# A decoder step on one core: norm weights spread by matmul, another load order for the first tile, bias rows read backwards, two small products moved later

## The chip, the cores and the metric

The kernel runs on one NeuronCore of one Trainium2 chip. Times are microseconds (us) of device time of one launch. The kernel before was run three times: 622.79, 621.86 and 620.78 us, median 621.86 us. One further execution was profiled.

## What is computed

The reference is one inference step of a hybrid decoder layer, on 512 prompt rows and 8 x 4 sample rows (544 rows in all, 1,024 wide). The part that the change touches is cut out here; after it come the gating mixer, the merge and the final norm.

```python
def rmsnorm(x, g):
    y = xf * lax.rsqrt(jnp.mean(xf * xf, axis=-1, keepdims=True) + EPS)
    return (y * g).astype(x.dtype)

h = rmsnorm(x, norm_g)                       # norm_g: 1024 weights
proj = jnp.einsum('bsd,de->bse', h, w_in)    # q, k, v, gates, ...
s_own = qf @ k_own + table_t[:, rel_bucket(pos_i[:, None] - own_pos[None, :])]
# causal attention of the prompt with a bias by distance (32 buckets per head)
# block-sparse attention of the sample rows over a paged cache, same table
```

## The kernel before, in words

All five engines run programs written out by hand; semaphores tie them together.

**The front (up to about 26 us).** The SP queue loads five row tiles of x (`XR`, 128 rows each, the last one 32 rows), and between them the norm weights copied to all 128 partitions (`GBC`, 512 KB, line 352), the constants (`CST`, line 353) and the first two pairs of weight tiles (`load_w(0)`, `load_w(1)`, 1 MB each). For each row tile r, ACT sums the squares (line 812), DVE makes the mean (`mean_square`, line 1011), POOL the inverse root (line 1399), DVE multiplies by it and by `GBC` (`normalise`, line 1018), PE transposes it in eight 128-column pieces (`turn_x(u)`, two u per tile, line 495), ACT copies the result out as `XH` (`x_hi`, called through line 799) and DVE makes the rest `XL` (`x_lo`, line 1027). Three tiles are made ready before the first projection half starts; `turn_x(6)` to `turn_x(9)`, tiles 3 and 4, are woven into that half. `turn_x(u)` waits for `x_lo` of u-4, whose PSUM bank it takes over. DVE's own order is ms(0), norm(0), ms(1), norm(1), ms(2), x_lo(0), norm(2), x_lo(1), x_lo(2), then tiles 3 and 4. Every weight tile is split in a high part `WH` (ACT, `split_hi`) and a low part `WL` (DVE, `split_lo`; for tiles 0 and 1 POOL, line 1409).

**The 12 tiles of q, k and v (26 to 112 us).** For tile n, PE runs `half(n, 0)`, then small extra work, then `half(n, 1)`. A half is 24 matmuls of 272 columns (line 455). ACT evicts each half. The extra work: at n=1 the table products; at n=5 to 11 `rows(n-1)`, five transposes of k or v; at n=5 and 6 two `flip` products each (line 517, FLIP x TREV, 128x512 f32), which ACT copies to `TPH`; at n=9 the local scores of the sample rows; at n=10 a wait for `loc_ok` and one product with `SUM` (line 553). `TREV` holds bias rows that POOL wrote to HBM and loads back with a step of one element per partition (lines 1411 to 1414). After the loop PE runs `rows(11)` and waits for `lmx_ok`.

**The steps (112 to about 500 us).** 144 steps t, ordered by hand: each transposes a page of keys (line 575), runs four k-steps of the remaining projection (`run(fill, 2)` twice) and adds page scores, page values and the pieces of prompt attention. `prompt_max` (DVE, lines 1177 to 1187) adds `TPH` to the scores in PSUM (line 1182) and takes the maximum; it runs 16 times, two adds each. The mixing, merge and final norm follow.

Of the kernel before, what the change touches and what calls it, by code (L numbers as in the profile page):

```python
# [8 lines left out]
F32 = mybir.dt.float32  # L9
# [71 lines left out]
C_ID, C_SUM, C_OWN, C_PAIR, C_TRI, C_FLIP = 0, 128, 256, 260, 262, 326  # L81
C_KEPT = 326
C_COLS = 454
# [6 lines left out]
def constants():  # L90

    c = np.zeros((P, C_COLS), np.float32)
    row, col = np.arange(P)[:, None], np.arange(P)[None, :]
    c[:, C_ID:C_ID + P] = np.eye(P)
    c[:, C_SUM:C_SUM + P] = row % 32 == col % 32
    c[:, C_FLIP:C_FLIP + P] = row + col == P - 1
# [7 lines left out]
    i[:, I_EVEC:I_EVEC + VLEN] = onehot([255 - u for u in range(VLEN)])  # L104
    i[:, I_VMASK:I_VMASK + VLEN] = np.where(np.arange(VLEN) > 255, NEG, 0.0)
# [39 lines left out]
def build(nc, x_p, x_s, cache_k, cache_v, page_table, rel_bias, norm_g, w_in, ln_g, ln_b, w_s, b_s, w_pa, w_pb,  # L145
          w_o, fin_g, cst, ini, sgc, y_p, y_s, k_p, v_p, k_s, v_s, sgu_s):
    with ExitStack() as ctx:
# [36 lines left out]
        CST = sb("CST", [P, C_KEPT])  # L184
# [46 lines left out]
        TREV = at("TREV", [P, NH, 2 * P], F32, o); o += NH * 2 * P * 4  # L231
        FLIP = at("FLIP", [P, P], F32, o); o += P * 4
# [46 lines left out]
        cst_ld, ini_ld, pt_ld, gbc_ld = sem("cst_ld"), sem("ini_ld"), sem("pt_ld"), sem("gbc_ld")  # L279
# [5 lines left out]
        tb_ok, tab_pe, tab_ok, vec_st, trev_ld = sem("tb_ok"), sem("tab_pe"), sem("tab_ok"), sem("vec_st"), sem("trev_ld")  # L285
        flip_ld, flip_pe, tph_ok = sem("flip_ld"), sem("flip_pe"), sem("tph_ok")
# [41 lines left out]
        def _(sp):  # L328
# [17 lines left out]
            for r in range(5):  # L346
                if r < 4:
                    sp.dma_start(XR[:, r, :], x_p[0, r * P:(r + 1) * P, :]).then_inc(x_ld[r], 16)
                else:
                    sp.dma_start(XR[0:NSR, r, :], x_s.rearrange("b t d -> (b t) d")).then_inc(x_ld[r], 16)  # L350
                if r == 0:
                    sp.dma_start(GBC[:], bass.AP(norm_g.tensor, norm_g.offset, [[0, P], [1, DM]])).then_inc(gbc_ld, 16)
                    sp.dma_start(CST[:], cst[:, 0:C_KEPT]).then_inc(cst_ld, 16)
                if r == 2:
                    load_w(0)
# [3 lines left out]
            sp.dma_start(FLIP[:], cst[:, C_FLIP:C_FLIP + P]).then_inc(flip_ld, 16)  # L359
# [84 lines left out]
        def _(pe):  # L444
# [41 lines left out]
            pe.wait_ge(cst_ld, 16)  # L486

            def turn_x(u):
                r, kk = u // 2, u % 2
                n = P if r < 4 else NSR  # L490
                wait(pe, xn_ok, r + 1)
                wait(pe, xt_lo, u - 3)
                for j in range(4):
                    k = 4 * kk + j
                    last = pe.transpose(BK[4 + u % 4][:, j * n:(j + 1) * n], XR[0:n, r, k * P:(k + 1) * P], IDN[0:n, 0:n])
                last.then_inc(xt_pe, 1)
# [12 lines left out]

            def flip(x):  # L510

                if x == 0:
                    pe.wait_ge(trev_ld, 16)
                    pe.wait_ge(flip_ld, 16)
                    pe.wait_ge(tab_ok, 1)
                wait(pe, tph_ok, x - 1)
                mm(BK[2 + x % 2][:], FLIP[:], TREV[:, 2 * x:2 * x + 2, :], start=True, stop=True).then_inc(flip_pe, 1)

# [3 lines left out]
            for n in range(N_QKV):  # L522
# [17 lines left out]
                if n in (5, 6):  # L540
                    flip(2 * (n - 5))
                    flip(2 * (n - 5) + 1)
                if n == 9:

                    pe.wait_ge(qc_ok, 4)
                    pe.wait_ge(tph_ok, 4)
                    for b in range(NB):
                        for c in range(PAIRS):
                            last = mm(BK[3][0:32, b * 32:(b + 1) * 32], QC[:, b, c, :], KTS[:, c, SEQ:ROWS], start=(c == 0), stop=(c == PAIRS - 1))
                    last.then_inc(loc_pe, 1)  # L550
                if n == 10:
                    pe.wait_ge(loc_ok, 1)
                    mm(BK[2][:, 0:NB], SUM, LMX0[:], start=True, stop=True).then_inc(lmx_pe, 1)
                run(half(n, 1))
            rows(N_QKV - 1)
# [173 lines left out]
            for t in range(STEPS):  # L729
                if t < PAGES:  # L730
                    turn_page(t)
                run(fill, 2)
                if t % 4 == 0 and 4 <= t <= PAGES:
                    page_scores(t // 4 - 1)
# [62 lines left out]
        def _(act):  # L797
# [3 lines left out]
            def split_hi(n):  # L801
                m = n // 2
                act.wait_ge(w_ld[m % 2], w_need(m))
# [18 lines left out]
            squares(1)  # L822
            x_hi(0)
            squares(2)
            x_hi(1)
            split_hi(0)
# [6 lines left out]
            for n in range(N_QKV):  # L833
# [146 lines left out]
        def _(dve):  # L980
# [25 lines left out]
            dve.wait_ge(zero_ok, 7)  # L1006
# [6 lines left out]
            def normalise(r):  # L1013
                n = P if r < 4 else NSR
                if r == 0:
                    dve.wait_ge(gbc_ld, 16)
# [50 lines left out]
            for n in range(N_QKV):  # L1067
# [13 lines left out]
                if n == 11:  # L1081
# [3 lines left out]
            rows_out(N_QKV - 1)  # L1085
# [88 lines left out]
            def prompt_max(i):  # L1174
# [3 lines left out]
                if i == 0:  # L1178
                    dve.wait_ge(tph_ok, 4)
# [107 lines left out]
            for t in range(STEPS):  # L1287
                n = N_QKV + t // 4
                if t % 4 == 0 and 4 <= t <= 128:
# [101 lines left out]
        def _(pool):  # L1391
# [9 lines left out]
            pool.wait_ge(zero_ok, 7)  # L1401
# [12 lines left out]
            pool.dma_start(TREV[:], bass.AP(vec_d.tensor, vec_d.offset, [[1, P], [VLEN, NH], [1, 2 * P]])).then_inc(trev_ld, 16)  # L1414
# [42 lines left out]
```

## Time and profile before

| | |
|---|---|
| three runs | 622.79, 621.86, 620.78 us (median 621.86) |
| profiled execution, its own time | 621.19 us |
| its span in the trace | 618.9 us |
| PE busy | 576.7 us (93%) |
| DVE, ACT, POOL busy | 314.6, 215.2, 33.1 us |
| DMA | 112.50 MB, mean 182 GB/s |

The execution's time is 2.3 us above its span; what lies around the span is the same program start and end in every run. A busy time is a sum over the span, and an engine that is not the bound may idle at no cost. The chain that ended last is followed back from the last instruction, at each step to what released it. Line numbers are those of the kernel before.

### The profile page before, as it was taken

What the parts mean: (1) busy time and instruction counts of PE and PEld (TensorE: products, weight loads), DVE (VectorE), ACT (ScalarE), POOL (GpSimd) and SP (SyncE); (2) the same over time, 40 slices, a digit from 0 to 9 for tenths busy, and PEclk for the clock granted to TensorE, in tenths of its full rate; (3) what the DMA queues carried; (4) which work ended last, traced back from release to release, by engine and by line L of the source; (5) the groups of instructions that cost most, each with busy time, mean ns of one, the idle gap of its engine ahead of it and who ended that gap; (6) DMA issues with size and microseconds to landing.
All of it is one profiled execution on the core that took longest, in us unless ns stands there. A gap on an engine that the chain in (4) does not pass through costs nothing.

```text
span 618.9 us, 15227 instructions
## 1 busy us (share of the span) xinstructions
PE 576.7 (93%) x6242; PEld 540.6 (87%) x6242; DVE 314.6 (51%) x695; ACT 215.2 (35%) x466; POOL 33.1 (5%) x42
## 2 busy tenths in 40 slices
PE   3899998999999999999999989999999999979990
PEld 2799998999899899999889978989999989979990
DVE  5532223436446555655855745873642455952306
ACT  5422322332433434444544442232443231323213
POOL 1310120100000000000000000020000001100002
PEclk9999999999999999999999999999999999989996
DMA  8337332564775866767658578786798572332003
GB/s 296 115 106 253 104 117 93 190 173 126 228 227 183 242 202 191 219 207 226 203 173 254 173 231 256 240 257 181 218 341 298 169 245 70 121 127 69 1 1 144
DMA packets 73990, 112.50 MB, mean 182 GB/s; under 512 B 5417, under 2 KB 38194, under 8 KB 73922
## 3 DMA queue, kind: packets, MB, share of 16 engines
q1 hardware_dynamic: 72690, 108.18, 55.1%
q0 software_dynamic: 1232, 3.36, 1.7%
q8 instruction: 50, 0.82, 0.6%
q14 instruction: 18, 0.15, 0.1%
HBM read 106.98 MB, written 4.53 MB: 180 GB/s over the span
## 4 chain that ended last, share of the span: by engine, by line
PE 75%; DVE 15%; ACT 5%; issue 3%; DMA 2%; SPq 0%; POOL 0%; DVEq 0%; ACTq 0%; POOLq 0%
PE BK L455 46%; PE BK L575 7%; PE BK L587 4%; PE BK L601 4%; PE BK L475 3%; PE BK L651 2%; DVE WL L997 2%; DVE G L1278 1%; PE BK L668 1%; PE BK L658 1%; ACT WH L799 1%; DVE XR L1018 1%; ACT SC L897 1%; ACT FJ L976 1%; DMA SGC<-in_gating_constants 1%
## 5 line engine op out<-in xcount | busy, mean ns | idle before, releaser
L455 PE MATMUL BK<-XH,WH 128*128 128x272 f32 x704 | 223.7, 318 | 1.4 <-DVE XL L1027 1.4
L455 PE MATMUL BK<-XH,WL 128*128 128x272 f32 x704 | 204.1, 290 | 0.0
L455 PE MATMUL BK<-XL,WH 128*128 128x272 f32 x704 | 203.0, 288 | 0.0
L455 PEld LDWEIGHTS BK<-XH,WH 128*128 128x128 f32 x704 | 133.2, 189 | 12.2 <-issue 9.2
L455 PEld LDWEIGHTS BK<-XL,WH 128*128 128x128 f32 x704 | 133.8, 190 | 0.5 <-issue 0.5
L455 PEld LDWEIGHTS BK<-XH,WL 128*128 128x128 f32 x704 | 133.1, 189 | 0.0
L997 DVE TENSOR_TENSOR WL<-WRAW,WH 128x1024 fp32r<-128x1024 f32 x56 | 68.6, 1224 | 100.7 <-ACT WH L799 100.6
L575 PE MATMUL BK<-CST,KRAW 128*128 128x128 f32 x512 | 77.1, 273 | 2.4 <-DVE ATS L1171 2.2
L1091 DVE COPY KT<-BK 128x512 f32<-128x512 f32 x64 | 44.2, 691 | 57.1 <-PE BK L575 57.0
L799 ACT ACTIVATE WH<-WRAW 128x1024 fp32r<-128x1024 f32 x60 | 63.2, 1053 | 18.0 <-PE BK L475 18.0
L575 PEld LDWEIGHTS BK<-CST,KRAW 128*128 128x128 f32 x512 | 60.2, 140 | 4.4 <-issue 4.1
L455 PE MATMUL BK<-MH,WH 128*128 128x272 f32 x128 | 37.8, 295 | 3.9 <-issue 3.9
L799 ACT ACTIVATE KT<-BK 128x512 f32<-128x512 f32 x64 | 38.1, 595 | 4.3 <-PE BK L575 3.1
L455 PE MATMUL BK<-MH,WL 128*128 128x272 f32 x128 | 37.6, 294 | 0.0
L455 PE MATMUL BK<-ML,WH 128*128 128x272 f32 x128 | 37.4, 292 | 0.0
L587 PE MATMUL BK<-KT,QC 128*32 128x128 f32 x1024 | 34.6, 276 | 0.0
L799 ACT ACTIVATE G<-BK 128x272 f32<-128x272 f32 x32 | 12.7, 397 | 62.3 <-PE BK L455 62.1
L601 PE MATMUL BK<-VRAW,PT 128*32 128x128 f32 x960 | 31.8, 273 | 0.1
L1399 POOL TENSOR_TENSOR RSTD<-MS,NHALF 128x1 f32<-128x1 f32 (+1 forms) x15 | 10.8, 722 | 373.0 <-DVE MS L1234 292.1
L587 PEld LDWEIGHTS BK<-KT,QC 128*32 128x32 f32 x1024 | 26.0, 109 | 4.8 <-issue 1.1
L910 ACT ACTIVATE APX<-BK,NMX 128x128 f32<-128x128 f32 (+3 forms) x32 | 16.6, 522 | 34.2 <-DVE NMX L1187 34.2
L455 PEld LDWEIGHTS BK<-MH,WH 128*128 128x128 f32 x128 | 24.8, 193 | 4.1 <-issue 4.1
(186 smaller groups left out, 776.6 us busy)
## 6 DMA issues: line engine op xcount, KB each, us to landing
KRAW<-in_cache_k SPq DMA_DIRECT2D x128, 256.0 KB, 3.5
VRAW<-in_cache_v SPq DMA_DIRECT2D x120, 256.0 KB, 3.7
WRAW<-in_w_in SPq DMA_DIRECT2D x22, 1024.0 KB, 5.7
WRAW<-in_w_o SPq DMA_DIRECT2D x4, 1024.0 KB, 5.1
XR<-in_x_prompt SPq DMA_DIRECT2D x4, 512.0 KB, 6.4
VEX<-in_cache_v SPq DMA_DIRECT2D x8, 256.0 KB, 4.6
WRAW<-in_w_pb SPq DMA_DIRECT2D x4, 512.0 KB, 6.8
WRAW<-in_w_pa SPq DMA_DIRECT2D x4, 512.0 KB, 5.2
```

The costliest lines, as they stand in the source:

```text
L455: last = mm(BK[h][:, 0:HALF], w[:, n % 2, k, :], x[:, k, cols], start=(k == 0 and w is WH and x is XA), stop=(k == KC - 1 and w is WL))
L475: last = mm(bank[:, 0:HALF], w[:, n % 2, 4 * x + k, :], y[:, k, cols], start=(k == 0 and w is WH and y is XA), stop=(k == 3 and w is WL))
L575: last = pe.transpose(BK[2 + i % 2][:, c * P:(c + 1) * P], KRAW[:, i % KR, c * P:(c + 1) * P], IDN)
L587: last = mm(SCB[32 * j:32 * j + 32, x * P:(x + 1) * P], QC[:, b, c, :], KT[:, (4 * q + j) % KB, c, :], start=(c == 0), stop=(c == PAIRS - 1))
L601: last = mm(OUT[32 * c:32 * c + 32, 0:P], PT[:, x, 32 * j:32 * j + 32], vals[:, c * P:(c + 1) * P], start=(p == 0), stop=False)
L651: last = mm(BK[6 + e][:, k0:k1], QT[hd, c, y * P:(y + 1) * P], KTS[hd, c, k0:k1], start=True, stop=True)
L658: last = pe.transpose(BK[6 + e][:, j * P:(j + 1) * P], APX[:, e, j * P:(j + 1) * P], IDN)
L799: return act.activation(o, i, ACT.Copy)
L910: act.activation(APX[:, e, 0:n], BK[6 + e][:, 0:n], ACT.Exp, bias=NMX[:, e:e + 1], scale=1.0 / UNIT, accum_out=PLS[:, e:e + 1]).then_inc(a ...
L997: dve.tensor_tensor(WL[:, n % 2], WRAW[:, n // 2 % 2, :, n % 2 * P:(n % 2 + 1) * P], f32(WH[:, n % 2]), ALU.subtract).then_inc(w_lo, 1)
L1091: dve.tensor_copy(KT[:, i % KB], BK[3][:].rearrange("p (c n) -> p c n", c=PAIRS)).then_inc(kt_dve, 1)
L1399: pool.tensor_tensor(RSTD[0:n, r:r + 1], MS[0:n, r:r + 1], NHALF[0:n], ALU.pow).then_inc(done, 1)
```

## The change

- `norm_g` is loaded once, as one row `GROW` of 4 KB on one partition. PE multiplies a column of ones with it (`ONE`, 1x128, against two halves of 1x512) into banks 6 and 7, DVE copies both to `GBC`. Both stand ahead of everything else on PE and DVE; `turn_x(2)` waits for the copies.
- The constants are loaded in two parts (identity early, the rest late). The loads are in the order x0, GROW, identity, x1, x2, first half of the first weight pair, x3, sample rows, the other half, `load_w(1)`, and the small tables.
- On ACT, `squares(2)` goes ahead of `x_hi(0)` and `split_hi(0)` ahead of `x_hi(1)`. On DVE, `x_lo(0)` goes behind `normalise(2)`.
- `FLIP`, `TREV` and the four flip products with their ACT copies are gone. The bias rows are written in the other order and loaded straight into `TPH`; `prompt_max` reads them with a step of -1.
- The `loc_ok` wait and the product with `SUM` go from n=10 to n=11, and `rows(11)` from the end of the loop into step 0, behind its first two k-steps; DVE's `rows_out(11)` goes with it.

```diff
-            for r in range(5):
-                ...
-                if r == 0:
-                    sp.dma_start(GBC[:], bass.AP(norm_g.tensor, norm_g.offset, [[0, P], [1, DM]])).then_inc(gbc_ld, 16)
-                    sp.dma_start(CST[:], cst[:, 0:C_KEPT]).then_inc(cst_ld, 16)
-                if r == 2:
-                    load_w(0)
+            def load_x(r):
+                sp.dma_start(XR[:, r, :], x_p[0, r * P:(r + 1) * P, :]).then_inc(x_ld[r], 16)
+            load_x(0)
+            sp.dma_start(GROW[:], norm_g).then_inc(g_ld, 16)
+            sp.dma_start(CST[:, 0:P], cst[:, 0:P]).then_inc(id_ld, 16)
+            load_x(1)
+            load_x(2)
+            c = COLUMN[0] * P
+            sp.dma_start(WRAW[:, 0, :, 0:P], w_in[0, :, c:c + P].rearrange("(k p) n -> p k n", p=P)).then_inc(w0_ld, 16)
+            load_x(3)
+            sp.dma_start(XR[0:NSR, 4, :], x_s.rearrange("b t d -> (b t) d")).then_inc(x_ld[4], 16)
+            sp.dma_start(WRAW[:, 0, :, P:2 * P], w_in[0, :, c + P:c + 2 * P].rearrange("(k p) n -> p k n", p=P)).then_inc(w_ld[0], 16)
             load_w(1)
             sp.dma_start(INI[:], ini).then_inc(ini_ld, 16)
             sp.dma_start(TAB[:], rel_bias).then_inc(ini_ld, 16)
-            sp.dma_start(FLIP[:], cst[:, C_FLIP:C_FLIP + P]).then_inc(flip_ld, 16)
+            sp.dma_start(CST[:, P:], cst[:, P:]).then_inc(cst_ld, 16)
...
-            pe.wait_ge(cst_ld, 16)
+            pe.wait_ge(g_ld, 16)
+            pe.wait_ge(zero_ok, 8)
+            for x in range(2):
+                last = mm(BK[6 + x][:], ONE[:], GROW[:, 512 * x:512 * x + 512], start=True, stop=True)
+            last.then_inc(gbc_pe, 1)
+            pe.wait_ge(id_ld, 16)
...
+                if u == 2:
+                    pe.wait_ge(gbc_ok, 1)
...
-                if n in (5, 6):
-                    flip(2 * (n - 5))
-                    flip(2 * (n - 5) + 1)
                 if n == 9:
                     pe.wait_ge(qc_ok, 4)
-                    pe.wait_ge(tph_ok, 4)
+                    pe.wait_ge(tab_ok, 1)
...
-                if n == 10:
+                if n == N_QKV - 1:
                     pe.wait_ge(loc_ok, 1)
+                    pe.wait_ge(cst_ld, 16)
                     mm(BK[2][:, 0:NB], SUM, LMX0[:], start=True, stop=True).then_inc(lmx_pe, 1)
                 run(half(n, 1))
-            rows(N_QKV - 1)
             pe.wait_ge(lmx_ok, 1)
...
                 run(fill, 2)
+                if t == 0:
+                    rows(N_QKV - 1)
...
             squares(0)
             squares(1)
+            squares(2)
             x_hi(0)
-            squares(2)
+            split_hi(0)
             x_hi(1)
-            split_hi(0)
...
-                if n in (5, 6):
-                    for x in (2 * (n - 5), 2 * (n - 5) + 1):
-                        act.wait_ge(flip_pe, x + 1)
-                        copy(TPH[:, 2 * x:2 * x + 2, :], BK[2 + x % 2][:].rearrange("p (h n) -> p h n", h=2)).then_inc(tph_ok, 1)
...
-            dve.wait_ge(zero_ok, 7)
+            dve.memset(ONE[:], 1.0).then_inc(zero_ok, 1)
+            dve.wait_ge(zero_ok, 8)
+            dve.wait_ge(gbc_pe, 1)
+            for x in range(2):
+                last = dve.tensor_copy(GBC[:, 512 * x:512 * x + 512], BK[6 + x][:])
+            last.then_inc(gbc_ok, 1)
...
             for r in range(3):
                 mean_square(r)
-                if r == 2:
-                    x_lo(0)
                 normalise(r)
+            x_lo(0)
             x_lo(1)
...
-                    add = dve.tensor_tensor(bk[:, n - w:n], bk[:, n - w:n], TPH[:, 2 * c + e, 2 * P - w:2 * P], ALU.add)
+                    bias = TPH[:, 2 * c + e, 0:w]
+                    add = dve.tensor_tensor(bk[:, n - w:n], bk[:, n - w:n], bass.AP(bias.tensor, bias.offset + w - 1, [list(bias.ap[0]), [-1, w]]), ALU.add)
...
-            pool.dma_start(TREV[:], bass.AP(vec_d.tensor, vec_d.offset, [[1, P], [VLEN, NH], [1, 2 * P]])).then_inc(trev_ld, 16)
+            pool.dma_start(TPH[:], bass.AP(vec_d.tensor, vec_d.offset + 1, [[1, P], [VLEN, NH], [1, 2 * P]])).then_inc(tph_ld, 16)
```

## Rows read from the trace of the kernel before

**Rows 1.** The page: busy time of PE, and its clock in 40 slices (tenths).

```profile
PE 576.7 (93%) x6242; PEld 540.6 (87%) x6242; DVE 314.6 (51%) x695; ACT 215.2 (35%) x466; POOL 33.1 (5%) x42
...
PEclk9999999999999999999999999999999999989996
```

**Rows 2.** The chain that ended last, 0 to 36 us: start us, us, what.

```profile
0.76 3.63 DMA XR<-in_x_prompt
...
6.63 1.29 DVE XR L1018
...
8.06 1.96 PE BK L495 x8
...
11.86 1.20 DVE XL L1027 x2
...
14.30 1.98 PE BK L495 x8
...
20.78 3.39 DVE XR L1018
...
25.96 6.99 PE BK L455 x54
```

**Rows 3.** Timeline of the front: start us, us, engine, line, operation [idle before, releaser].

```profile
1.21 0.42 SPq L352 DMA_DIRECT2D GBC<-in_norm_g  x1
...
8.16 1.06 ACT L812 ACTIVATE JUNK<-XR 128x1024 f32<-128x1024 f32 x1 [2.60 <-DMA XR<-in_x_prompt]
...
9.34 0.15 DVE L1011 TENSOR_SCALAR MS<-SS 128x1 f32<-128x1 f32 x1 [1.42 <-ACT JUNK L812]
...
10.16 1.28 DVE L1018 SCALAR_TENSOR_TENSOR XR<-XR,RSTD,GBC 128x1024 f32<-128x1024 f32 x1 [0.67 <-POOL RSTD L1399]
...
14.00 1.05 ACT L799 ACTIVATE WH<-WRAW 128x1024 fp32r<-128x1024 f32 x1
...
17.68 0.59 PE L455 MATMUL BK<-XH,WH 128*128 128x272 f32 x1 [1.41 <-DVE XL L1027]
...
20.72 2.35 POOL L1409 TENSOR_TENSOR WL<-WRAW,WH 128x1024 fp32r<-128x1024 f32 x1
```

**Rows 4.** Two matmuls of the projection before 20 us and two after 24.5 us, same timeline.

```profile
18.08 0.43 PE L455 MATMUL BK<-XL,WH 128*128 128x272 f32 x1
...
18.30 0.43 PE L455 MATMUL BK<-XH,WL 128*128 128x272 f32 x1
...
24.80 0.29 PE L455 MATMUL BK<-XL,WH 128*128 128x272 f32 x1
...
24.93 0.29 PE L455 MATMUL BK<-XH,WL 128*128 128x272 f32 x1
```

**Rows 5.** DMA issues, 0 to 70 us: KB each, us from issue to landing.

```profile
GBC<-in_norm_g SPq DMA_DIRECT2D x1, 512.0 KB, 5.2
...
TAB<-in_rel_bias SPq DMA_DIRECT2D x1, 1.0 KB, 9.0
...
vec_scratch<-VEC POOLq DMA_DIRECT2D x1, 12.0 KB, 1.9
```

**Rows 6.** The chain again, 54 to 72 us, around the flip products.

```profile
59.94 1.72 PE BK L517 x4
...
68.25 1.72 PE BK L517 x4
```

**Rows 7.** Timeline of DVE at 60 us: a copy of one PSUM bank.

```profile
59.97 0.69 DVE L1060 COPY RS<-BK 128x512 f32<-128x512 f32 x1 [0.98 <-PE BK L508]
```

**Rows 8.** Who PE waited for, 56 to 125 us: us in total, times, longest.

```profile
PE BK L553 <- DVE LMX L1080: 1.7, 1, 1.7
PE BK L507 <- issue: 0.5, 1, 0.5
```

**Rows 9.** Line 1182, duration ns min/median/max; and the chain, 186 to 200 us.

```profile
L1182 DVE TENSOR_TENSOR BK<-BK,TPH x32: 289/423/433, 154.3 to 344.3; 128x256 f32<-128x256 f32 x24, 128x128 f32<-128x128 f32 x8
...
191.59 0.77 DVE BK L1182 x2
```

More of the change, by code:

```diff
@@ L78, in onehot @@
     return e
-C_ID, C_SUM, C_OWN, C_PAIR, C_TRI, C_FLIP = 0, 128, 256, 260, 262, 326
-C_KEPT = 326
-C_COLS = 454
+C_ID, C_SUM, C_OWN, C_PAIR, C_TRI = 0, 128, 256, 260, 262
+C_COLS = 326
 I_E15, I_ELOC, I_EVEC, I_VMASK, I_LOCM = 0, 512, 640, 1024, 1408
@@ L95, in constants @@
     c[:, C_SUM:C_SUM + P] = row % 32 == col % 32
-    c[:, C_FLIP:C_FLIP + P] = row + col == P - 1
     c[:, C_OWN:C_OWN + 4] = np.arange(4)[None, :] == row // 32
@@ L103, in constants @@
         i[:, I_ELOC + t * 32:I_ELOC + (t + 1) * 32] = onehot([t - j for _ in range(NB) for j in range(TD)])
-    i[:, I_EVEC:I_EVEC + VLEN] = onehot([255 - u for u in range(VLEN)])
-    i[:, I_VMASK:I_VMASK + VLEN] = np.where(np.arange(VLEN) > 255, NEG, 0.0)
+    i[:, I_EVEC:I_EVEC + VLEN] = onehot([u - P for u in range(VLEN)])
+    i[:, I_VMASK:I_VMASK + VLEN] = np.where(np.arange(VLEN) < P, NEG, 0.0)
     m = np.full((NH, TD, NB, NB, TD), NEG, np.float32)
@@ L183, in build @@
         TG = sb("TG", [P, 2, ROWS])
-        CST = sb("CST", [P, C_KEPT])
+        CST = sb("CST", [P, C_COLS])
         PTB = sb("PTB", [1, PAGES], I32)
@@ L230, in build @@
         VEC = at("VEC", [NH, VLEN], F32, o); o += VLEN * 4
-        TREV = at("TREV", [P, NH, 2 * P], F32, o); o += NH * 2 * P * 4
-        FLIP = at("FLIP", [P, P], F32, o); o += P * 4
+        GROW = at("GROW", [1, DM], F32, o); o += DM * 4
+        ONE = at("ONE", [1, P], F32, o); o += P * 4
         assert o <= g_at + 24 * ROWS * 4
@@ L278, in build @@
         x_ld = [sem(f"x_ld{r}") for r in range(5)]
-        cst_ld, ini_ld, pt_ld, gbc_ld = sem("cst_ld"), sem("ini_ld"), sem("pt_ld"), sem("gbc_ld")
+        id_ld, cst_ld, ini_ld, pt_ld, g_ld, w0_ld = (sem(n) for n in ("id_ld", "cst_ld", "ini_ld", "pt_ld", "g_ld", "w0_ld"))
+        gbc_pe, gbc_ok = sem("gbc_pe"), sem("gbc_ok")
         w_ld = [sem("w_ld0"), sem("w_ld1")]
@@ L284, in build @@
         xt_pe, xt_hi, xt_lo = sem("xt_pe"), sem("xt_hi"), sem("xt_lo")
-        tb_ok, tab_pe, tab_ok, vec_st, trev_ld = sem("tb_ok"), sem("tab_pe"), sem("tab_ok"), sem("vec_st"), sem("trev_ld")
-        flip_ld, flip_pe, tph_ok = sem("flip_ld"), sem("flip_pe"), sem("tph_ok")
+        tb_ok, tab_pe, tab_ok, vec_st, tph_ld = sem("tb_ok"), sem("tab_pe"), sem("tab_ok"), sem("vec_st"), sem("tph_ld")
         w_hi, w_lo, pj = sem("w_hi"), sem("w_lo"), sem("pj")
@@ L344, in load_w @@
                     sp.dma_start(WRAW[:, slot], w_in[0, :, c:c + 2 * P].rearrange("(k p) n -> p k n", p=P)).then_inc(w_ld[slot], 16)
-            for r in range(5):
[L347 to L350, printed above, removed]
-                if r == 0:
-                    sp.dma_start(GBC[:], bass.AP(norm_g.tensor, norm_g.offset, [[0, P], [1, DM]])).then_inc(gbc_ld, 16)
-                    sp.dma_start(CST[:], cst[:, 0:C_KEPT]).then_inc(cst_ld, 16)
-                if r == 2:
-                    load_w(0)
+            def load_x(r):
[10 more added lines that the diff above has]
+            sp.dma_start(WRAW[:, 0, :, P:2 * P], w_in[0, :, c + P:c + 2 * P].rearrange("(k p) n -> p k n", p=P)).then_inc(w_ld[0], 16)
             load_w(1)
@@ L508, in rows @@
                 pe.transpose(bs[0:NSR, 0:P], src[:, SEQ:ROWS], IDN).then_inc(rows_pe, 1)
[L510 to L517, printed above, removed]
             for u in range(6):
@@ L802, in split_hi @@
                 m = n // 2
-                act.wait_ge(w_ld[m % 2], w_need(m))
+                if n == 0:
+                    act.wait_ge(w0_ld, 16)
+                else:
+                    act.wait_ge(w_ld[m % 2], w_need(m))
                 wait(act, pj, matmuls_before(n - 1) if n > 1 else 0)
@@ L1015, in normalise @@
                 if r == 0:
-                    dve.wait_ge(gbc_ld, 16)
+                    dve.wait_ge(gbc_ok, 1)
                 dve.wait_ge(rstd_ok, r + 1)
@@ L1080, in _ @@
                     dve.tensor_reduce(LMX0[0:32, :], LOCS[:], AX.X, ALU.max).then_inc(loc_ok, 1)
-                if n == 11:
+                if n == N_QKV - 1:
                     dve.wait_ge(lmx_pe, 1)
@@ L1084, in _ @@
                 split_lo(n + 2)
-            rows_out(N_QKV - 1)
             def page_out(i):
@@ L1178, in prompt_max @@
                 if i == 0:
-                    dve.wait_ge(tph_ok, 4)
+                    dve.wait_ge(tph_ld, 16)
                 for e in range(2):
                     bk = BK[6 + e]
-                    add = dve.tensor_tensor(bk[:, n - w:n], bk[:, n - w:n], TPH[:, 2 * c + e, 2 * P - w:2 * P], ALU.add)
+                    bias = TPH[:, 2 * c + e, 0:w]
+                    add = dve.tensor_tensor(bk[:, n - w:n], bk[:, n - w:n], bass.AP(bias.tensor, bias.offset + w - 1, [list(bias.ap[0]), [-1, w]]), ALU.add)
                 link(add)
@@ L1288, in _ @@
                 n = N_QKV + t // 4
+                if t == 0:
+                    rows_out(N_QKV - 1)
                 if t % 4 == 0 and 4 <= t <= 128:
@@ L1399, in inverse_root @@
                 pool.tensor_tensor(RSTD[0:n, r:r + 1], MS[0:n, r:r + 1], NHALF[0:n], ALU.pow).then_inc(done, 1)
-            pool.wait_ge(zero_ok, 7)
+            pool.wait_ge(zero_ok, 8)
             for r in range(5):
```

## The prediction

> **What bounds the kernel now.** I read the page first. PE is busy for 93% of the span, and the clock line shows 9 tenths or more in nearly every slice [rows 1], so from about 26 us on anything that takes PE instructions away, or an idle gap of PE, should come off the time almost one for one, and work on DVE, ACT or POOL matters only where PE waits for it. The exception is the start. I followed the chain of waits there and then the timeline beside it: until the first projection matmul at 17.68 us [rows 3] the chain goes load of the first x tile, squares, root, norm on DVE, transposes on PE, and again [rows 2]. PE is mostly idle there; the last wait of the front is for the norm of the sample rows (3.39 us from 20.78), and from 25.96 us PE runs without a gap [rows 2]. A change of the front counts only by what it does to this chain. The other two views are the chain around the flip products [rows 6] and the list of what PE waited for up to 125 us, which has just two entries in the stretch that the change touches [rows 8].
>
> **Term 1, the flip products.** Each of the two groups stands on the chain with 1.72 us [rows 6], between two runs of line 455. Removing them gives 2 x 1.72 = 3.44 us. Their four ACT copies and the two loads they needed (FLIP, and TREV, which becomes TPH with the same bytes on the same POOL queue) were beside PE. PE's new wait at n=9 is for `tab_ok`, which DVE gives eight tiles earlier, behind the table products of n=1; it holds nothing up.
>
> **Term 2, the later product with SUM.** PE stood 1.7 us for `LMX` at n=10 [rows 8], because the product was asked for right behind `rows(9)`, while DVE still had to copy the rows, add the scores and reduce. One tile later DVE has had a whole half (6 us, 48 matmuls in the same view) for it. The product itself stays. What is late next: DVE copies `LMX` at n=11, and PE needs `lmx_ok` only after another half, 24 matmuls. Gain 1.7 us.
>
> **Term 3, `rows(11)` later.** It waited 0.5 us for ACT's eviction [rows 8]. Behind two k-steps of filling that eviction is long done. DVE's `rows_out(11)` had `split_lo(13)` before it anyway, so PE's delay of the five transposes does not show there. Gain 0.5 us.
>
> **Term 4, the front.** The loads get lighter: 512 KB of copied norm weights become 4 KB. But loads were not what the chain waited for after the second squares (the load of x1 ended its wait at 8.16 us [rows 3]). What is new is that nothing may be normalised before GROW has landed, PE has made two products and DVE has copied two banks, and DVE's first `mean_square` is queued behind these copies, POOL's root behind that. Step by step:
>
> - GROW is issued where GBC was, at 1.21 us [rows 3], right behind x0, which took 3.63 us from issue to landing and was down at 4.39 [rows 2]. GBC itself, in this place and with 512 KB, took 5.2 us [rows 5]. The ends of the range are the 1.9 us of a small store from an idle POOL queue and the 9.0 us of the 1 KB load of TAB [rows 5]. I take 3.5 us, between x0 and the small store but nearer to x0, since it shares x0's queue: landed at 4.7.
> - Two products of 512 f32 columns. The same two-product group costs 1.72 us in the flips [rows 6], at PE's upper level. In the front PE runs at the lower one (1.2 GHz of 2.4): neighbouring matmuls start 0.22 us apart at 18 us and 0.13 us apart at 24.8 us [rows 4], and before that it had only short bursts between waits. The granted clock in the page's line does not show this, so I go by the pace. Ends 1.72 and 3.44; PE has done nothing at all before, so 3.44: done at 8.3 with the drain.
> - Two copies of a bank, 0.69 us each [rows 7]: done at 9.7.
> - `mean_square` to the start of the norm takes 0.82 us (9.34 to 10.16 [rows 3]); the first norm starts at 10.5, where it started at 6.63 before [rows 2].
> - DVE now does three such rounds without a break: 1.28 us of norm and 0.82 us less a small overlap, about 2.05. Squares are ready, since x1 and x2 land earlier. The third norm starts at 14.6 and ends at 15.9. Before `turn_x(4)` can start, `x_lo(0)` has to free its bank: 0.6 us for its first piece (1.20 for two [rows 2]), so 16.6 us. Before the change those transposes started at 14.30 [rows 2].
>
> That is 2.3 us later. From there the order is what it was (transposes, `x_hi(2)`, squares of tiles 3 and 4, roots, norms), each released by the one before, so the first matmul moves from 17.68 to about 20.0 and the gapless run from 25.96 to about 28.3. The first weight half is loaded ahead of x3 and behind 0.5 MB less than before, so it is there earlier, and is split while DVE norms. Cost 2.3 us.
>
> **Term 5, the backward read.** Line 1182 takes 0.289 us for 128 columns and 0.423 for 256 [rows 9], so 1.05 ns an element. No row has a negative step. Lower bound of the cost 0 (a gain is excluded, the elements are as many); upper, one more such time per element. I take 0, as the add already reads PSUM and SBUF streams at one rate in any stride that the rows show. Of the 16 calls, the four with the full 512 rows of scores lie on the chain, two adds each (one of them is 191.59, 0.77 us [rows 9]), so the upper end is 8 x 256 x 1.05 ns = 2.1 us.
>
> **Sum.** -3.44 - 1.7 - 0.5 + 2.3 = -3.4 us (rounded). The profiled execution took 621.19 us and would become 617.8. It lies 0.67 under the median of three; the mean of the four executions is 621.66, and against that I forecast **618.2 us**. This main case can be off by a microsecond to each side from GROW's landing, and by as much from when PE's clock rises: in the first half, matmuls before 24 us are nearly 0.1 us apiece dearer, and a rise a little earlier or later than before is paid there. Its own range is 616.8 to 619.7. A measurement of this kernel can tell about 0.3%, 1.9 us, from no change.
>
> **The rivals.**
>
> - **PE is at its upper level for the products** (or GROW lands as fast as the small store): 1.7 us less in term 4, 616.5 us. For it: nothing; against it: 8 transposes in 1.96 us at 8.06 [rows 2], against which the products come earlier still. Chance 0.10. The Trainium skill (TensorE: Matmul & The Clock Gate, What's actually happening) says the throttled state is the default and activity releases it; by that rule the products run at the lower level, and the trace agrees in that the matmuls at 18 us have the slow pace.
> - **POOL gets in front of the third norm.** At 20.72 POOL starts its 2.35 us subtraction `WL` [rows 3] and DVE's norm at 20.78 takes 3.39 us instead of 1.28 [rows 2]: it ends one norm after POOL does. `split_hi(0)` (ACT, 1.05 us, 14.00 before [rows 3]) now stands ahead of `x_hi(1)`, so the first `WL` could be ready just as the third norm starts, right behind the third root on the same POOL. By my times ACT is done at about 15.6, a microsecond after the norm's start at 14.6, so the norm wins. If the transposes are faster or the norm later, it loses 2.1 us: 620.3. Chance 0.10. The Trainium skill (SBUF — State Buffer, Who interferes with whom) has it that a DVE instruction with two SBUF inputs and a GpSimd instruction that reads SBUF lock each other out and whoever starts first holds the ports; the trace agrees with 3.39 against 1.28 us.
> - **The backward read is slower**, by one more 1.05 ns an element: 2.1 us, 620.3. For it: no row excludes it; against: the operation has PSUM on both sides and no fast mode to lose. Chance 0.10.
> - **Slower than before: GROW lands late.** Where TAB's 1 KB took 9.0 us [rows 5], it stood behind all of x, GBC and two weight pairs in the queue; if one packet to one partition behaves so here too, it lands at 10.2, 5.5 us later than I take. PE, DVE and POOL all wait, and the whole chain of the front shifts with it: 618.2 + 5.5 = 623.7 us. It decides from a landing at 8.1 us on (there the time is as before); slower by 0.3% needs 10. Against it: x0 alone is ahead of it, down at 4.39. Chance 0.08.
>
> That the change does not do what it says is hardly possible for terms 1 to 3: the instructions are gone or moved behind work that lasts longer than the wait.
>
> **How the numbers follow.** Main case 0.62. Faster by over 0.3%: main and the first rival, 0.72. Within 0.3%: POOL's lock and the backward read, 0.20. Slower: 0.08. The range from 616.2 to 620.6 takes in the first three rivals' values and the bounds of terms 4 and 5, and leaves out the late GROW.
>
> **What would show it.** Right: no line of FLIP; no wait for `LMX`; `rows(11)` without idle time; two products on PE of some 1.7 us each at about 4.7 us; the first norm at 10.5, the first line-455 matmul near 20.0 and the gapless run from 28.3; line 1182 still at 423 ns. Wrong: a first norm before 9 us (then I overpriced products or landing), a third norm of over 3 us (the lock), adds of 0.6 us and more, or a new idle entry of PE between 28 and 125 us.

## The result, and the profile after

The changed kernel takes 619.65 us in the median of 20 runs (616.13 to 621.09), the kernel before 622.92 us in the median of 20 (620.73 to 625.27, the three of the front among them). The ratio is 0.994, 95% interval 0.9922 to 0.9957: faster by 3.3 us between the medians and by 3.7 us by the ratio. The forecast was 618.2 us and 3.4 us faster; it started from 621.66 us for the kernel before, 1.3 us under the median of the 20. The profiled execution of the changed kernel took 616.13 us, the lowest of its 20; its span is 614.0 us against 618.9, 4.9 us less.

The page of the changed kernel, busy time and PE's clock, to be held against [rows 1]:

```profile
PE 575.8 (94%) x6238; PEld 539.5 (88%) x6238; DVE 315.6 (51%) x698; ACT 213.2 (35%) x462; POOL 33.3 (5%) x42
...
PEclk9799999999999999999999999999999999989996
```

PE has four instructions fewer (eight of the flips gone, four of GROW's products new). The clock line has a 7 in its second slice that was not there before.

The chain that ended last in the changed kernel, 0 to 38 us (start us, us, what), against [rows 2]. `normalise` is line 1022 here, `turn_x` line 505, the half 457, the products of ones and GROW 492, the copies 1009:

```profile
1.22 3.21 DMA GROW<-in_norm_g
...
4.47 3.79 PE BK L492 x4
...
8.36 1.29 DVE GBC L1009 x2
...
10.52 1.28 DVE XR L1022
...
14.54 1.28 DVE XR L1022
15.83 0.61 DVE XL L1031
...
16.58 0.65 PE BK L505 x4
...
22.32 3.39 DVE XR L1022
...
27.54 7.00 PE BK L457 x54
```

Read it from the top: the new path (load of GROW, products, copies) is the chain until 9.65 us, then three norms in close order. Where the chain names neither product nor norm it runs through a mean (line 1015), a root (POOL, line 1404) or `x_lo` (line 1031). The first norm starts at 10.52 us where it started at 6.63, the last one at 22.32 where it was 20.78, and the gapless run at 27.54 where it was 25.96. The front has lost 1.58 us.

The chain again, 100 to 115 us, where the two small products stand (line 552 is the product with SUM, 573 a page's transposes, 517 and 518 `rows`):

```profile
102.76 0.44 PE BK L517 x4
103.20 0.11 PE BK L518
103.31 0.12 PE BK L552 x2
103.44 3.12 PE BK L457 x24
106.55 0.44 PE BK L573 x4
106.99 0.76 PE BK L457 x6
107.75 0.44 PE BK L517 x4
108.18 0.11 PE BK L518
108.29 0.75 PE BK L457 x6
109.04 0.44 PE BK L573 x4
```

No piece says "issue" and no other engine stands in it: both waits of [rows 8] are gone. The product with SUM takes 0.12 us between matmuls; before, alone behind a wait, 0.39 us passed from its start to the next matmul of the half. A good place to compare the kernels is the start of page 1's transposes, which ends the stretch that the change touches: 113.49 us before, 108.88 after by PE's timeline. From the gapless run to page 1 it is 87.53 us before and 81.34 after, 6.19 us less. The parts: 3.44 for the flips, 1.74 + 0.27 for the SUM product, and 0.73 for `rows(11)` (3.22 us from the end of the half at 110.43 to page 1 at 113.65 in the chain of the kernel before; 2.49 now, from 106.55 to 109.04), 6.18 together. With the 1.58 us of the front that is 4.6 us; the remaining 0.3 to 0.4 us of the 4.9 comes in the steps (370.98 us from page 1 to the last page before, 370.62 now).

And the add with the backward read (durations ns min/median/max), to be held against [rows 9]:

```profile
L1185 DVE TENSOR_TENSOR BK<-BK,TPH x32: 289/423/433, 149.7 to 340.0; 128x256 f32<-128x256 f32 x24, 128x128 f32<-128x128 f32 x8
```

The three numbers are those of before.

### The profile page after: what moved, and what is told of

Read it like the earlier page. It is cut to its first block, busy times and chain, and to the rows that moved or that the text cites. A ratio compares the mean times of both kernels' runs of the same rounds, so it can differ in the third digit from the quotient of the medians.

```text
span 614.0 us, 15221 instructions
## 1 busy us (share of the span) xinstructions
PE 575.8 (94%) x6238; PEld 539.5 (88%) x6238; DVE 315.6 (51%) x698; ACT 213.2 (35%) x462; POOL 33.3 (5%) x42
## 3 DMA queue, kind: packets, MB, share of 16 engines
q0 software_dynamic: 1232, 3.36, 1.9%
## 4 chain that ended last, share of the span: by engine, by line
PE 78%; DVE 14%; ACT 4%; issue 3%; DMA 1%; POOL 0%; DVEq 0%; SPq 0%; ACTq 0%; POOLq 0%
PE BK L457 48%; PE BK L573 8%; PE BK L585 4%; PE BK L599 4%; PE BK L477 3%; PE BK L649 2%; DVE G L1281 1%; DVE WL L996 1%; PE BK L666 1%; PE BK L656 1%; DVE XR L1022 1%; ACT SC L896 1%; ACT FJ L975 1%; ACT WH L799 1%; DVE G L1279 1%
```

## The experiments

Theory: the flips and the waits come off one for one, and the new front gives part of it back because GROW, products and copies are on its chain. The main rival is that the front's price or gain is not from that path but from the order of loads and of ACT, or from PE's clock.

### 1. The norm weights by DMA again

```diff
-            sp.dma_start(GROW[:], norm_g).then_inc(g_ld, 16)
+            sp.dma_start(GBC[:], bass.AP(norm_g.tensor, norm_g.offset, [[0, P], [1, DM]])).then_inc(g_ld, 16)
...
-            for x in range(2):
-                last = mm(BK[6 + x][:], ONE[:], GROW[:, 512 * x:512 * x + 512], start=True, stop=True)
...
-                last = dve.tensor_copy(GBC[:, 512 * x:512 * x + 512], BK[6 + x][:])
```

> The changed kernel with one thing undone: the norm weights come by the old 512 KB load into GBC, in GROW's place in the queue; no products, no copies, everything else as changed. Theory (the GROW-products-copies path holds the front back, and the front goes into the end one for one): the first norm starts at about 6.6 us instead of 10.52, the third norm ends between 12.5 and 13.5 instead of 15.83 (x1 and x2 land a little later than in the changed kernel), and the gapless run of the projection starts 2 to 3 us before the changed kernel's 27.54, so about 2 us off the end: ratio to the kernel before near 0.990 against 0.994. Rival (the front is held by something else, the order of ACT or the loads of x, and the products cost nothing): the gapless run starts at 27 to 28 us as in the changed kernel, ratio 0.994.

Measured: 615.67 us (6 runs), ratio 0.9888 (0.9857 to 0.9918). Its chain in the front (line 1011 is the norm, 498 `turn_x`):

```profile
2.15 6.14 DMA XR<-in_x_prompt
...
12.32 1.28 DVE XR L1011
...
20.81 3.38 DVE XR L1011
...
24.24 0.63 PE BK L498 x4
24.87 1.66 PE BK L457 x6
26.53 0.56 PE BK L498 x4
27.09 7.93 PE BK L457 x54
```

The first norm starts at 6.67 us, the third ends at 13.60, the first projection matmul starts at 17.71 instead of 19.48, and the last norm at 20.81 instead of 22.32. So GROW's path did hold the front back. By the times it cost 4.0 us between the medians, 3.2 by the ratios. But in the profiled execution (616.18 us, 0.5 above its median) the gapless run starts at 27.09, only 0.45 us earlier, where 2 to 3 were expected. One part of the miss is that the 3.9 us of the first norm have shrunk to 1.5 by the last. The other: behind the last norm the same pieces take 0.63, 1.66 and 0.56 us that take 0.47, 0.95 and 0.36 us in the changed kernel, and the 54 matmuls 7.93 instead of 7.00. PE is at its lower level there, by these durations. This was the first sight of something that the forecast had only as a width.

### 2. The old front with everything else

The kernel before with the flips, `TREV` and `FLIP` taken out as in the change, and the late products:

```diff
-                if n in (5, 6):
-                    flip(2 * (n - 5))
-                    flip(2 * (n - 5) + 1)
...
-                if n == 10:
+                if n == N_QKV - 1:
                     pe.wait_ge(loc_ok, 1)
...
-            rows(N_QKV - 1)
...
+                if t == 0:
+                    rows(N_QKV - 1)
...
-                    add = dve.tensor_tensor(bk[:, n - w:n], bk[:, n - w:n], TPH[:, 2 * c + e, 2 * P - w:2 * P], ALU.add)
+                    bias = TPH[:, 2 * c + e, 0:w]
+                    add = dve.tensor_tensor(bk[:, n - w:n], bk[:, n - w:n], bass.AP(bias.tensor, bias.offset + w - 1, [list(bias.ap[0]), [-1, w]]), ALU.add)
```

> The front of the kernel before, unchanged (old loads, GBC by DMA, old order on ACT and DVE), with the rest of the change: no flip products, backward bias, the SUM product and rows(11) later. Theory (PE is the bound behind the front): page 1's transposes start 3.44 + 1.74 + 0.27 + 0.73 = 6.2 us earlier than before (113.65 -> about 107.5), and the whole is 6 us faster, ratio 0.990. Rival (part of what the changed kernel wins comes from its front, for instance through the clock of PE): less than 5 us, ratio 0.992 or more.

Measured: 616.94 us (6 runs), ratio 0.9896 (0.9869 to 0.9922); first projection matmul at 17.71 us, as in experiment 1, so the new order of loads and of ACT by itself gives nothing there; the times do not tell the two kernels apart either (0.9896 and 0.9888). The chain behind the last norm (line 491 `turn_x`, 451 the half):

```profile
20.70 3.39 DVE XR L999
...
24.13 0.63 PE BK L491 x4
24.76 1.66 PE BK L451 x6
26.42 0.56 PE BK L491 x4
26.98 8.05 PE BK L451 x54
```

This front is the kernel before's, instruction for instruction in the part shown, and ends its last norm within 0.1 us of it, yet the gapless run starts 1.02 us later and its first 54 matmuls take 8.05 us against 6.99 [rows 2]: 2.1 us lost to the lower level. PE's work up to there is the same in both, so I put it down to chance of the execution; one profile of each cannot show more. Page 1 is at 109.37, 4.1 us earlier than before, and with the 2.1 us back it is the 6.2 us of the theory. The times agree with that: 6.0 us between the medians. The rival (less than 5 us, a ratio of 0.992 or more) is left only the upper end of the interval.

The whole span is only 2.9 us shorter, because there is a second such place, which the change does not touch. In every one of these kernels PE stands idle for 3.9 us once between 536 and 550 us, and its granted clock falls to 0.50. Over 540 to 560 us the mean granted clock is 0.83 here and in experiment 3, and 0.91 in the kernel before and the changed kernel; from page 1 to the end the former two take 506.6 and 506.5 us, the latter two 505.4 and 505.1.

### 3. The two late products alone

```diff
-                if n == 10:
+                if n == N_QKV - 1:
                     pe.wait_ge(loc_ok, 1)
...
-            rows(N_QKV - 1)
             pe.wait_ge(lmx_ok, 1)
...
+                if t == 0:
+                    rows(N_QKV - 1)
```

> The kernel before with the two late products alone (the SUM product at n = 11, rows(11) in step 0). Theory: page 1's transposes start 1.74 + 0.27 + 0.73 = 2.7 us earlier (113.65 -> about 110.9), ratio 0.9955. Rival (the stall only moves to the wait for lmx_ok or to DVE's rows_out(11) in the steps): page 1 at 112.5 or later, or a wait for lmx_ok or for KT that was not there, ratio above 0.998.

Measured: 620.03 us (12 runs), ratio 0.9958 (0.9935 to 0.9981). PE waits for nothing between 56 and 130 us. Page 1 is at 112.73, only 0.8 us earlier, which by itself would be the rival's sign (112.5 or later). But no new wait is there, and here too PE was at the lower level in the profiled execution (gapless run from 27.09 us, 54 matmuls in 7.84): 1.13 and 0.85 us, and 0.76 + 1.13 + 0.85 is 2.7. The ratio, over twelve runs, says the same 2.6 us.

### 4. The bias part alone

The diff is experiment 2's without its two hunks on `loc_ok` and `rows`.

> The kernel before with the bias part alone: no FLIP, no flip products, TPH loaded straight and read with a step of -1. Theory: page 1's transposes 3.44 us earlier for the same start of the projection, ratio 0.9945, and line 1182's operation at 423 ns as before. Rival (the steps give it back, since DVE or the loads bound them): page 1 earlier by 3.4 us but the last page by less than 2.

Measured: 618.42 us (8 runs), ratio 0.9936 (0.9911 to 0.996). The gapless run starts at 26.07 us, page 1 at 110.13, so 3.47 us less between them than before. The steps keep it: from page 1 to the last page 370.8 us, before 371.0. The rival is out.

### 5. The first mean ahead of DVE's wait

```diff
-                last = mm(BK[6 + x][:], ONE[:], GROW[:, 512 * x:512 * x + 512], start=True, stop=True)
-            last.then_inc(gbc_pe, 1)
+                mm(BK[6 + x][:], ONE[:], GROW[:, 512 * x:512 * x + 512], start=True, stop=True).then_inc(gbc_pe, 1)
...
-            dve.wait_ge(gbc_pe, 1)
+            dve.wait_ge(ss_ok, 1)
+            dve.tensor_scalar(MS[0:P, 0:1], SS[0:P, 0:1], 1.0 / DM, EPS, ALU.mult, ALU.add).then_inc(ms_ok, 1)
             for x in range(2):
+                dve.wait_ge(gbc_pe, x + 1)
...
-                mean_square(r)
+                if r > 0:
+                    mean_square(r)
```

> The changed kernel with mean_square(0) ahead of DVE's wait for the products (so that POOL's root runs beside them) and each copy released by its own product. Theory (DVE's head of queue is part of the price): the first norm starts at about 9.1 us (second product done 8.26, its copy 0.7, no mean and root behind it) instead of 10.52, and the first projection matmul follows 1.4 us earlier (19.48 -> 18.1); ratio a quarter per cent under the changed kernel's 0.994. Rival (the mean and root are hidden behind something else, the squares of x1 or the load of x2): the third norm ends at 15.8 as now.

Measured: 616.36 us (6 runs), ratio 0.99 (0.9873 to 0.9927).

```profile
4.45 3.79 PE BK L492 x4
...
8.26 0.70 DVE GBC L1010
...
8.99 1.28 DVE XR L1023
```

The first norm starts at 8.99 us, the third at 13.02, the first projection matmul at 17.95: 1.53 us gained by moving the mean ahead of the wait and letting each copy wait for its own product only. The gapless run starts at 26.04 us, 1.50 earlier. The head of DVE's queue was part of the price, as step 4 of the forecast had it.

### 6. The products twice

```diff
+            for x in range(2):
+                mm(BK[6 + x][:], ONE[:], GROW[:, 512 * x:512 * x + 512], start=True, stop=True)
             for x in range(2):
                 last = mm(BK[6 + x][:], ONE[:], GROW[:, 512 * x:512 * x + 512], start=True, stop=True)
```

> The changed kernel with the two products of ones and GROW made twice over. Theory (they are on the chain of the front, at PE's lower level, 0.86 us an instruction): the first norm starts between 12.2 (if PE's clock rises during them) and 13.9 us instead of 10.52, and the first projection matmul moves from 19.48 by the same 1.7 to 3.4 us. Rival (the products run beside something as long): the first norm stays within 0.5 us of 10.52.

Measured: 622.25 us (10 runs), ratio 0.9992 (0.9974 to 1.0011). The first norm starts at 14.06 us, 3.54 later, the first projection matmul at 23.01, 3.53 later, the gapless run at 31.11, 3.57 later. One for one, and it eats the whole gain. The second four instructions took 3.43 us on the chain, 0.86 each: PE's pace did not rise in 7 us of them. The 14.06 is 0.2 us past the upper end that I had given.

### 7. POOL ahead of the third norm

```diff
-            x_hi(0)
             split_hi(0)
+            x_hi(0)
             x_hi(1)
```

> The changed kernel with ACT's split_hi(0) ahead of x_hi(0), so that POOL can start its first WL right behind the third root, at the moment when DVE starts the third norm. Theory of the lock: the third norm takes 3.4 us instead of 1.28 (or POOL's WL waits 1.3 us, if the norm is first), and in the first case the first projection matmul comes about 2 us later than 19.48. Rival (no lock; the 3.39 us of the last norm have another cause, such as its 32 partitions): the third norm takes 1.28 us and POOL's WL 2.35, both at once.

Measured: 621.14 us, a single execution. The timeline at the third norm, in the kernel's own lines (1414 POOL's WL, 1022 the norm):

```profile
14.48 2.35 POOL L1414 TENSOR_TENSOR WL<-WRAW,WH 128x1024 fp32r<-128x1024 f32 x1
14.55 3.36 DVE L1022 SCALAR_TENSOR_TENSOR XR<-XR,RSTD,GBC 128x1024 f32<-128x1024 f32 x1 [0.66 <-POOL RSTD L1404]
```

POOL starts 0.07 us before DVE, and DVE's norm ends 1.08 us after POOL does: 3.36 us instead of 1.28. The first projection matmul is at 21.97 us, 2.49 later, and the gapless run starts 2.9 us later, at 30.43. By the Trainium skill (SBUF — State Buffer, Who interferes with whom) whoever starts first of a DVE instruction with two SBUF inputs and a GpSimd instruction that reads SBUF keeps the other out for the whole instruction; the trace agrees. The lock that the forecast had as a rival exists; the changed kernel's third norm misses it, since its WL starts at 15.55, one microsecond into the norm. Its last norm does not: WL starts at 22.26, the norm at 22.32 and takes 3.38 us, as in the kernel before.

### 8. PE kept busy, and the last norm out of the lock

By now the front looked like this: the last norm, held by POOL's second WL, hides until 24 us that PE works at its lower level, and whether the level is up by then differs between executions. So on top of experiment 1:

```diff
+            def keep_busy(count):
+                for _ in range(count):
+                    mm(BK[2][:, 0:P], zq[:, 0:P], zq[:, P:2 * P], start=True, stop=True)
...
+            keep_busy(10)
...
+                keep_busy({1: 7, 3: 6, 5: 8}.get(u, 0))
...
+                        if u == 6:
+                            keep_busy(8)
...
                     if n:
                         pool.wait_ge(w_lo, n)
+                        pool.wait_ge(xn_ok, 5)
```

The products of zeros are extra work whose result nobody reads.

> The kernel of e1 (GBC by DMA) with two additions: POOL's second WL waits until the last norm is done, and PE fills its gaps in the front with 39 products of zeros (128x128, into a bank that nobody reads yet). Theory (in the front PE is at its lower level, and when it rises differs from run to run; the last norm's 3.4 us hide this until 24 us): PE is at the upper level by 17.7 us, the last norm ends near 22.2 instead of 24.2, the gapless run of the projection starts at 23 to 24 us instead of 27.09, and the times spread less than 2 us; ratio 0.984 or less. Rival (products of zeros don't raise the clock, or the level doesn't matter): the run starts at 26 us or later, ratio as e1's 0.989 or worse by the products' own time.

Measured: 612.2 us (5 runs, 611.47 to 612.71), ratio 0.9827 (0.9805 to 0.9849). The chain at the end of the front (line 516 is the products of zeros, 497 `turn_x`):

```profile
19.61 0.44 PE BK L497 x4
20.05 0.38 PE BK L457 x3
...
22.92 0.36 PE BK L497 x4
23.28 6.99 PE BK L457 x54
```

Four transposes in 0.44 us and three matmuls in 0.38 is the upper level; no norm is in this stretch of the chain any more. The gapless run starts at 23.28, 4.3 us earlier than in the changed kernel, and the five times lie within 1.24 us. Twenty of the changed kernel spread over 4.96 and twenty of the kernel before over 4.5; but even six executions each of experiments 1, 2 and 5 spread over 3.4 to 3.9 us.

Which of the two additions did it, and whether GROW's path still costs anything, the last four runs ask. The first is experiment 1 with the `xn_ok` line alone, the second experiment 1 with `keep_busy` alone. The third is the kernel with both additions and four products of zeros fewer,

```diff
-                keep_busy({1: 7, 3: 6, 5: 8}.get(u, 0))
+                keep_busy({1: 7, 3: 6, 5: 6}.get(u, 0))
...
-                            keep_busy(8)
+                            keep_busy(6)
```

and the fourth is the changed kernel with the `xn_ok` line and, defined as above, 22 products of zeros:

```diff
+            keep_busy(8)
             pe.wait_ge(id_ld, 16)
...
+                keep_busy({1: 0, 3: 2, 5: 6}.get(u, 0))
...
+                            keep_busy(6)
```

> e1 with POOL's second WL behind the last norm, without the products of zeros. Theory (PE's level is the other half of it): the last norm takes 1.28 us and ends near 22.1, but PE, at its lower level, is busy with tile 3 and the first k-steps until 24.0 to 24.2, so the gapless run starts at 25.9 to 27.1 as in e1; ratio 0.988 to 0.989. Rival (the lock alone was the price, and e13's gain is its end): the run starts at 24 to 25, ratio near 0.985.

> e1 with the 39 products of zeros alone, POOL's second WL where it was. Theory: the last norm takes 3.4 us again and ends at 23.4 (22.1 plus the lock, less what PE's level gives before), so the gapless run starts near 25.2, always at the upper level: 1 to 2 us better than e1, 2 us worse than e13, ratio 0.986, spread under 2 us. Rival (the level gave nothing): ratio and spread as e1.

> e13 with two products of zeros fewer in the two last gaps, where they outlasted the gap by 0.2 to 0.3 us. Theory: the gapless run starts at 23.0 instead of 23.28, ratio 0.982. Rival (fewer products let the level fall again): a slow pace in the first half and 1 us or more lost.

> The changed kernel as it is (GROW, products, copies) with 22 products of zeros in PE's gaps behind its own products and with POOL's second WL late. Theory (PE's level and the lock cost both fronts alike; what the GROW path costs stays): the first norm starts at 10.5 as before, the first projection matmul near 19.3, the gapless run at 25.0 to 25.5, 1.8 to 2 us behind e13's; ratio near 0.986. Rival (GROW's products repay their price by raising the level): within 0.5 us of e13.

| kernel | median us (runs) | ratio, interval | last norm us | gapless run from |
|---|---|---|---|---|
| GBC by DMA (1) | 615.67 (6) | 0.9888, 0.9857 to 0.9918 | 3.37 | 27.09 |
| (1) and POOL late | 615.0 (4) | 0.9886, 0.9851 to 0.9921 | 1.27 | 26.42 |
| (1) and PE busy | 614.79 (4) | 0.9873, 0.984 to 0.9906 | 3.39 | 25.50 |
| (1) and both | 612.2 (5) | 0.9827, 0.9805 to 0.9849 | 1.27 | 23.28 |
| (1) and both, four products of zeros fewer | 611.99 (6) | 0.9832, 0.9808 to 0.9857 | 1.27 | 23.33 |
| changed kernel, both | 614.81 (6) | 0.9878, 0.9853 to 0.9903 | 1.27 | 25.63 |

With POOL late alone the norm is short, but PE is still in its slow transposes when it ends. The chain of that kernel:

```profile
20.08 1.12 PE BK L498 x4
21.20 0.68 PE BK L457 x3
21.88 0.85 PE BK L498 x4
22.73 1.36 PE BK L457 x6
24.09 0.56 PE BK L498 x4
24.65 1.41 PE BK L457 x6
```

With PE busy alone, PE is fast until 21.7 us and then stands 1.85 us for the norm, which ends at 23.5:

```profile
23.55 0.43 PE BK L497 x4
...
24.93 0.56 PE BK L497 x4
25.50 8.23 PE BK L457 x54
```

Behind that gap its clock falls: the granted clock is 1.00 from 22 to 24 us, 0.71 from 24 to 26 and 0.50 from 26 to 28, and the 54 matmuls take 8.23 us instead of 6.99. I had expected the upper level throughout; the 25.50 of the table looks 1.24 us better than it is. So the locked-out norm costs twice, by the wait and by the level that PE loses in it. Of the two limits either covers most of the other: taking away the lock alone gives 0.7 us between the medians and keeping PE busy alone 0.9, and by the ratios neither stands clear of the intervals; only both together give the 3.5 us between the medians of 1 and 8. The trimmed version is no faster (I expected 0.3 us): the products of zeros had not been in the way. The last two rows and the two with one addition were measured beside a kernel before of 621.6 us, the others beside 622.9, so across these the ratios compare better than the medians.

The last row answers the question of the change. Once PE's level is settled and the lock gone, the kernels with GROW's path and with the 512 KB load differ in that path and in how many products of zeros fill the gaps, and the gapless run is 2.35 us later with GROW (25.63 against 23.28, first norm at 10.57 against 6.66); the medians differ by 2.6 us, and by 2.8 between the last two rows, which were measured side by side. (The two profiled spans, 613.4 and 609.3 us, differ by more, since the kernel with GROW had the longer fall between 540 and 560 us, with a granted clock of 0.83 against 0.92.) The 2.35 us is a little more than the 1.8 to 2 us that I had expected. GROW's products do not repay their price.

## Why the prediction was right, and where it was not

The mechanism holds term by term. That the sum comes so near (3.4 us against 3.3 to 3.7) is luck in part: what PE no longer does or waits for gave 6.2 us and not 5.64 (experiment 2), and by the times the front cost more than forecast, 2.7 us between the ratios of experiment 2 and of the changed kernel against 2.3. The two errors have opposite signs. The sum itself has a slip: its terms add up to 3.34, which is 618.3 us and not 618.2. And where term 2 speaks of a whole half for DVE, it is a whole tile, two halves, that its 48 matmuls and 6 us stand for.

- **Flip products.** 3.44 us forecast; 3.47 us measured in experiment 4, and nothing given back.
- **Product with SUM.** 1.7 us forecast, 2.0 found: the wait itself is the 1.74; I took the product as unchanged, but behind a wait 0.39 us passed until the next matmul, and in the stream it is 0.12.
- **`rows(11)`.** 0.5 us forecast, 0.73 found, for the same kind of reason: the restart behind the idle time is cheaper too. Both products together: 2.7 us, experiment 3.
- **The front, step by step.** GROW landed at 4.43 us (I took 4.7), the products were done at 8.26 (8.3), the copies at 9.65 (9.7), the first norm started at 10.52 (10.5), the third ended at 15.83 (15.9), the transposes behind it began at 16.58 (16.6). Then it came out better than forecast: those eight transposes took 1.23 us in place of the 1.98 of [rows 2], since PE was at its upper level for them, and the first projection matmul came at 19.48 instead of 20.0. In this execution the front cost 1.58 us and not 2.3. When PE's level is settled, GROW's path costs 2.35 us (experiment 8). The step's mechanism, a chain through GROW, PE and the head of DVE's queue, is shown by experiments 1, 5 and 6.
- **Backward read.** Cost 0 forecast and found: 289/423/433 ns twice.
- **What was undervalued: the clock.** I had put it down as a microsecond to either side. The kernels of experiments 2 and 3 lost 2.0 to 2.1 us to it in one execution with the front of the kernel before, and the kernels without it and without the lock spread by 1.2 us (five executions), 0.9 and 1.6 (six each). The profiled executions of both kernels were lucky ones: in both the level was up right behind the last norm. The changed kernel's was the luckier, 3.5 us under its median where the other is 1.7 under its own; this is why the difference of the spans, 4.9 us, is more than that of the times, 3.3 to 3.7 us. Whether the changed kernel meets the slow case more often than the kernel before, which the times would suggest (eleven of its 20 lie between 619.2 and 621.1 us, eight between 616.1 and 617.9, one at 618.9), stays open: no profile of such a slow execution of it was taken. The mean granted clock on record does say that they ran otherwise than the profiled one: the five executions at 0.981 to 0.983, the profiled one among them, took 616.1 to 617.9 us, the three at 0.988 took 617.2 to 617.3, and the twelve at 0.986 and 0.987 took 618.9 to 621.1.
- **Rivals.** GROW landing late did not happen, nor a slow backward read. POOL's lock is real (experiment 7) and the third norm missed it by a microsecond, as forecast. PE at its upper level for the products did not happen either, even for eight instructions in a row.

## What to carry to other kernels

Price a setup path by its position in each engine's queue, not by its bytes: a 4 KB load with two products and two copies cost more than the 512 KB load that it replaced, because it stood at the head of PE and DVE and the chain of the norms began behind it, while the big load had been hidden. A small product that waits for a slow chain belongs one tile later. And where a front has two limits of the same length, here a locked-out norm and a slow PE, removing one shows next to nothing: try both together before calling either harmless.

## What was not expected of the hardware

When PE first reaches its full pace differs between executions, and the granted clock tells it only in part. With the same front it was there at 24.2 us in the kernel before, and in experiments 1 to 3 it came only between 28.8 and 29.1. Windows of the changed kernel (us; busy time and instructions of PE, PEld, DVE, ACT, POOL; granted clock; DMA share, GB/s):

```profile
12.00:16.00 4.00, 3.81 (x16) 3.06 (x16) 2.80 (x4) 2.67 (x5) 1.50 (x3) 1.00 1.14 314
...
18.00:20.00 2.00, 0.52 (x2) 0.53 (x3) 1.57 (x4) 1.91 (x4) 0.31 (x2) 0.77 0.15 33
20.00:22.00 2.00, 0.86 (x5) 0.54 (x4) 1.34 (x2) 1.66 (x3) 0.55 (x2) 0.50 0.00 0
22.00:24.00 2.00, 2.00 (x12) 2.00 (x10) 1.68 (x1) 0.60 (x1) 2.00 (x2) 0.50 0.00 0
24.00:26.00 2.00, 1.92 (x11) 1.60 (x10) 2.00 (x2) 0.60 (x1) 0.62 (x1) 0.53 0.12 22
26.00:28.00 2.00, 2.00 (x18) 1.77 (x17) 1.21 (x4) 0.56 (x2) 0.00 (x0) 1.00 0.99 316
```

From 20 to 24 us of the changed kernel the granted clock is 0.50, the lower level of 1.2 GHz, and the matmuls have the slow pace; from 26 us it is 1.00, 2.4 GHz, and they have the fast one. But at 12 to 16 us it also says 1.00 while 16 transposes take 3.8 us, the slow pace. So before the first rise the column is no witness and the durations are. What went before the fall is the gap in PE's work between 17.8 and 19.5 us; before the rise PE was busy from 21.7 us nearly without a break. The 1.85 us gap of the kernel with PE busy alone was followed by a fall in the same way. The Trainium skill (TensorE: Matmul & The Clock Gate, What's actually happening) has the throttled state as the default from which activity releases; experiment 8 agrees, with products of zeros as the activity: 1.00 and the fast pace from the first transposes at 8.1 us on (eight in 1.06 us against 1.96 [rows 2]). There too the column reads 1.00 from the start, so it is the pace that shows it: the first ten products of zeros, two instructions each, took 4.48 us for the 20, the next seven 1.73 us for 14.
